# Re-pitching the state stage of a two-layer trunk: eight pairs of channel blocks, four weight tiles apart

## What is computed

```python
u = (h @ w_in)
bu = complex(einsum('blgc,gpc->blgp', ug, real(b_bar)), einsum('blgc,gpc->blgp', ug, imag(b_bar)))
_, s = associative_scan(_lin_combine, (a, bu), axis=1)
y = einsum('blgp,gcp->blgc', real(s), c_re) - einsum('blgp,gcp->blgc', imag(s), c_im)
y = y.reshape(bsz, seq, S5_WIDTH) + d * u
val, gate = split(gelu(y) @ w_out, 2, axis=-1)
x = x + val * sigmoid(gate)
```

## Time and profile before

| | us |
|---|---|
| median of 3 runs | 2246.61 (2244.24 to 2249.15) |
| the profiled execution | 2250.04 |
| its span, first to last instruction | 2248.0 |
| TensorE busy in the span | 2229.2 |
| VectorE busy | 1442.2 |
| ScalarE busy | 1021.1 |
| 1200 to 1300 us: TensorE, VectorE busy | 95.55, 83.50 |

### The profile page before, as it was taken

How to read it: one execution, slowest core, us unless ns; L and a number is a source line. 1 busy time by engine, 2 the same in 40 slices (tenths; PEclk the granted TensorE clock), 3 DMA queues, 4 the chain that set the end, 5 groups by cost and what they waited for, 6 DMA issues and landing times.

```text
span 2248.0 us, 28342 instructions
## 1 busy us (share of the span) xinstructions
PE 2229.2 (99%) x11250; PEld 1834.4 (82%) x11250; DVE 1442.2 (64%) x1590; ACT 1021.1 (45%) x1233; POOL 494.0 (22%) x469
## 2 busy tenths in 40 slices
PE   9999999999999999999999999999999999999998
PEld 7888878888888888888887788888888888888886
DVE  7878776667666666666668766555555445555665
ACT  5544454444434444445444455444444344444444
POOL 1245236455665544301003100000000000000001
PEclk9999999999999999999999999999999999999999
DMA  8667799888887888887779877677766667777764
GB/s 288 188 206 232 242 274 269 245 245 254 248 247 219 259 259 245 249 256 265 236 250 338 302 220 222 198 222 217 217 213 214 191 195 221 219 215 232 227 213 143
DMA packets 348517, 527.90 MB, mean 235 GB/s; under 512 B 105968, under 2 KB 125312, under 8 KB 347744
## 3 DMA queue, kind: packets, MB, share of 16 engines
q1 hardware_dynamic: 337296, 488.50, 71.4%
q0 software_dynamic: 8320, 30.75, 3.8%
q10 hardware_dynamic: 2768, 6.83, 0.9%
HBM read 474.10 MB, written 51.90 MB: 234 GB/s over the span
## 4 chain that ended last, share of the span: by engine, by line
PE 90%; DVE 4%; DMA 3%; issue 1%; ACT 1%; SPq 1%; DVEq 0%; ACTq 0%
PE PS L1566 58%; PE PS L1572 29%; DVE WLO L1057 1%; DMA HT<-zd 1%; DMA RAW<-in_s_w_out 1%; DMA RAW<-in_ffn_w 1%; ACT WHI L779 0%; PE PS L1597 0%; DMA RAW<-in_s_w_in 0%; PE PS L1669 0%; PE PS L1837 0%; PE PS L1838 0%; PE PS L1836 0%; DVE CB L1469 0%; PE PS L1660 0%
## 5 line engine op out<-in xcount | busy, mean ns | idle before, releaser
L1566 PE MATMUL PS<-WHI,OP 128*128 128x512 f32 x6208 | 1541.3, 390 | 1.4 <-ACT WHI L779 1.1
L1057 DVE TENSOR_TENSOR WLO<-RAW,WHI 128x1024 fp32r<-128x1024 f32 x783 | 1022.2, 1317 | 660.8 <-ACT WHI L779 657.9
L1566 PEld LDWEIGHTS PS<-WHI,OP 128*128 128x128 f32 x6208 | 1161.7, 188 | 248.1 <-issue 6.6
L779 ACT ACTIVATE WHI<-RAW 128x1024 fp32r<-128x1024 f32 x783 | 825.4, 1061 | 936.0 <-PE PS L1572 759.6
L1572 PE MATMUL PS<-WLO,OP 128*128 128x512 f32 x3104 | 830.7, 389 | 3.8 <-DVE WLO L1057 3.6
L1572 PEld LDWEIGHTS PS<-WLO,OP 128*128 128x128 f32 x3104 | 582.2, 188 | 127.1 <-DVE WLO L1057 6.1
L763 POOL TENSOR_TENSOR ON<-X,GF 128x1024 f32<-128x1024 f32 x3 | 9.9, 3291 | 947.8 <-DVE X L1406 947.8
L666 POOL TENSOR_TENSOR TA<-BRAW,FAC 128x64 f32<-128x64 f32 x16 | 8.2, 512 | 259.8 <-DMA BRAW<-in_s_b_im 259.8
L1069 DVE TENSOR_TENSOR OP<-HT,OP 128x512 fp32r<-128x512 f32 x50 | 34.9, 739 | 46.7 <-ACT OP L794 46.7
L794 ACT ACTIVATE OP<-HT 128x512 fp32r<-128x512 f32 x50 | 28.8, 624 | 65.3 <-DMA HT<-zd 65.3
L827 ACT ACTIVATE S<-PS,RC 128x512 f32<-128x512 f32 x66 | 41.8, 685 | 36.5 <-PE PS L1572 36.5
(11 more groups left out here) (213 smaller groups left out, 961.6 us busy)
## 6 DMA issues: line engine op xcount, KB each, us to landing
RAW<-in_ffn_w SPq DMA_DIRECT2D x528, 512.0 KB, 4.7
RAW<-in_gm_w_in SPq DMA_DIRECT2D x64, 512.0 KB, 4.7
RAW<-in_ple_w_gate SPq DMA_DIRECT2D x64, 512.0 KB, 4.8
RAW<-in_s_w_out SPq DMA_DIRECT2D x64, 512.0 KB, 5.2
zd<-ZT SPq DMA_DIRECT2D x37, 512.0 KB, 4.1
HT<-zd SPq DMA_DIRECT2D x148, 128.0 KB, 5.5
RAW<-in_gm_w_out SPq DMA_DIRECT2D x32, 512.0 KB, 5.3
RAW<-in_s_w_in SPq DMA_DIRECT2D x32, 512.0 KB, 6.1
```

What stands on the lines that cost most here:

```text
L779: A_.activation(hi_of(t), RAW[:, t % RING, :], ACT.Copy).then_inc(hi_ready, 1)
L1057: V_.tensor_tensor(lo_of(t), RAW[:, t % RING, :], hi_of(t).bitcast(F32), ALU.subtract).then_inc(lo_ready, 1)
L1566: T_.matmul(dst[:, th, :], x_part, WHI[:, slot, f], start=first and kk == 0 and part == 0, stop=False)
```

## The change

The eight duos had their increments 3, 5, 3, 5, 2, 6 and 2 tiles apart, and their outputs likewise. Now they stand four apart: increments at tiles 16, 20, 24, 28, 32, 36, 40, 43 and outputs at 20, 24, 28, 32, 36, 40, 44, 47. So for d = 1 to 6 the increments of duo d come right behind the outputs of duo d-1, behind the same tile. The outputs still come four tiles behind the increments of the same duo. The loads of the tables move with them, those of the last three duos' `TD` and `TK` by one to four tiles later. In `EARLY` step 4 of columns 0 and 1 goes to tiles 40 and 41 (it was at 44 and 45), and column 2 begins at tile 42 instead of 40. No instruction is added or taken away.

```diff
-EARLY = [(n, j) for j in range(4) for n in (0, 1)] + [(2, j) for j in range(4)]
-EARLY += [(n, j) for j in range(4, 8) for n in (0, 1, 2)]
+EARLY = [(n, j) for j in range(5) for n in (0, 1)] + [(2, j) for j in range(5)]
+EARLY += [(n, j) for j in range(5, 8) for n in (0, 1, 2)]
...
-INTO_AT = [W0 + g for g in (16, 19, 24, 27, 32, 34, 40, 42)]
-OUT_AT = [W0 + g for g in (20, 23, 28, 31, 36, 38, 44, 46)]
+INTO_AT = [W0 + g for g in (16, 20, 24, 28, 32, 36, 40, 43)]
+OUT_AT = [W0 + g for g in (20, 24, 28, 32, 36, 40, 44, 47)]
...
-TD_AT += [(W0 + g, W0 + g + 1) for g in (22, 26, 30, 37, 39)]
-TK_AT += [(W0 + g, W0 + g + 1) for g in (24, 30, 32, 39, 41)]
+TD_AT += [(W0 + g, W0 + g + 1) for g in (22, 26, 34, 38, 41)]
+TK_AT += [(W0 + g, W0 + g + 1) for g in (24, 30, 36, 40, 43)]
```

More of the change, by code:

```diff
@@ L183 @@
 TE_AT = [G0 + 12, G0 + 26]
-TQ_AT += [(W0 + g, W0 + g + 1) for g in (17, 20, 25, 28, 33, 35)]
-TD_AT += [(W0 + g, W0 + g + 1) for g in (22, 26, 30, 37, 39)]
-TK_AT += [(W0 + g, W0 + g + 1) for g in (24, 30, 32, 39, 41)]
-TE_AT += [W0 + g for g in (20, 23, 28, 31, 36, 38)]
+TQ_AT += [(W0 + g, W0 + g + 1) for g in (17, 21, 25, 29, 33, 37)]
+TD_AT += [(W0 + g, W0 + g + 1) for g in (22, 26, 34, 38, 41)]
+TK_AT += [(W0 + g, W0 + g + 1) for g in (24, 30, 36, 40, 43)]
+TE_AT += [W0 + g for g in (20, 24, 28, 32, 36, 40)]
 def set_before(d):
```

## The result

| | before | after |
|---|---|---|
| median, us | 2246.45 (2244.24 to 2251.0, 10 runs) | 2256.51 (2253.41 to 2258.61, 10 runs) |
| ratio | | 1.0039, 95% interval 1.003 to 1.0047 |
| the profiled execution | 2250.04 | 2257.53 |
| its span | 2248.0 | 2255.8 |

The change costs time, and +5.6 us was forecast. The medians differ by 10.1 us; the ratio, which is not that of the two medians, says 8.8, its interval 6.7 to 10.6. The busy times of the page hardly differ from the earlier trace rows (TensorE 2227.6 us, VectorE 1443.5); it counts 28344 instructions in all, two more than before, though none was added by hand.

The account below looks back on a forecast made before the run. TensorE, busy 2229.2 of 2248.0 us, was taken as the bound. New losses of 13.7 us, less 7.2 lost before, less 0.9 from joining, gave +5.6 us: 2252.2 on the median 2246.61, range 2243.5 to 2258.

Parts of the forecast that it names:

- the rival of the late loads: Table and weight loads share queue bandwidth; at 12 us a load each loop lengthens, giving 2256 to 2258 us; chance 0.13.
- The loop of VectorE: VectorE's work per duo takes 14.85 us, 16.05 with a column's transpose, against TensorE's 14.3, so VectorE falls back.
- Joining: Six pairs of outputs and increments become one group each on TensorE, saving 0.15 us a pair, 0.9 us gained.
- The walk: State stage followed in time: TensorE waits 0.8 us at tile 32, 1.1 at tile 36 and 8.0 at tile 40.
- 7 was named as a sign: On ScalarE, the spread of columns 2 and 3 comes 7 us after its store, two high parts between.
- The clock: TensorE's clock drops after the wait at tile 40; 3.4 us at half rate lose 1.7 us, ends 0 and 3.4.
- The outputs of duo 6: TensorE waits there for the transpose of the last scan: 2.1 us, between 0 and 3.
- New losses together: TensorE's new waits and low clock in the state stage: 0.8 + 1.1 + 8.0 + 1.7 + 2.1 = 13.7 us.
- 7.2 us "lost before": TensorE's loss between tile 16 and the last outputs in the old pitch: 117.3 us for 110.1 of work, taken back.
- VectorE keeps pace: Rival: the loop is nearer 14.3 us, the wait at tile 40 is 4.3; 2244.1 to 2246.2 us; chance 0.22.
- the even pitch pays: Rival: duo 4's output is ready within 9.4 us, all 7.2 and 0.9 go, 2238.5 us; chance 0.07.

Follow-up runs that it names:

- e11: The changed kernel with long-met waits added on TensorE ahead of the 100 tiles before W0; 2253.16 against 2246.76 us, ratio 1.0034.
- e3: The changed kernel with VectorE's transpose of each output ahead of the next scan, low and high passes also earlier; 2244.13 against 2245.47 us, ratio 0.9998.
- e10: e3 with two long-met waits added on TensorE ahead of each of 100 earlier tiles; 2243.66 against 2244.94 us, ratio 0.9996.
- e1: The changed kernel with step 4 of out1's columns 0 and 1 taking duo 3's output instead of duo 4's; 2252.12 against 2245.47 us, ratio 1.003.
- e7: The changed kernel with no group joined, output chain ahead of the scan, outputs taken ahead of spreads; 2244.32 against 2245.11 us, ratio 0.9993.
- e8: e3 with the outputs of duo 3 one tile earlier, so one joined group less; 2248.16 against 2245.11 us, ratio 1.0011.
- e4: The changed kernel with increments of duos 1, 3 and 5 one tile earlier, so half the groups are joined; 2252.31 against 2245.47 us, ratio 1.0032.
- e2: The kernel before with only the new order of the first columns, its old pitch kept; 2246.32 against 2245.47 us, ratio 1.0002.

## Why the prediction came out as it did

The sign, the mechanism and the place were right; the size was +10.1 us by the medians, +8.8 by the ratio, for +5.6. The median, 2256.51, lies inside the range, but 1.5 us above what the forecast gave by itself (2249.5 to 2255) and where the rival of the late loads was put (2256 to 2258). That rival is not what happened, so the number alone would point to the wrong case.

- **The loop of VectorE** (Part 2): 16 and 15, 16.5 and 15 us apart were forecast, 15.85, 14.69, 15.91 and 14.71 measured. A chain across two engines that work in order was priced from rows of before to within 0.6 us.
- **Joining**: the clean group takes 4.12 from 1198.11 to 1202.23, less 0.91 is 3.21, and 0.17 for the longer high part behind it (1.98 from 1202.23 to 1204.21, where 1.81 is usual) 3.38, against 3.56 apart: 0.18 saved, not 0.15. By the rule of the Trainium skill, "TensorEngine Tiling (Array Packing)", section "Key Properties", a drain at each change of mode, the prediction's estimate was 0.12. The trace agrees rather with a group paying once on entry and once on leaving: 1.01 us from L1775 to L1783 and 1.09 on to L1758, as in a group apart.
- **The walk** (Part 3): tiles 32 and 36 were not waited for (0.8 and 1.1 forecast), and tile 40 for 6.0 rather than 8.0. Here a step was missing: TensorE's pauses, 2.4 us from start to start of what lies around them from duo 2 on, made it come later to a chain that didn't wait for it. Wait and pauses are 8.4, for 9.9 forecast. The store on ScalarE also held less than thought: it landed in 5.9 us at the median and not 7.6, and the spreads came 6.3 us behind it for column 2 and 5.6 for column 3, where 7 was named as a sign.
- **The clock**: 2.0 for 1.7, though the second trace of after lost 2.9 by it. **The outputs of duo 6**: 2.2 for 2.1.
- **New losses together**: 6.0 + 2.4 + 0.7 (the pause in duo 1's increments) + 2.0 + 2.2 = 13.3, for 13.7 forecast; joining gave 1.1, for 0.9.
- **The term that failed is the 7.2 us "lost before".** The walk was made against the one trace, and against that trace it holds: 13.3 less 7.2 less 1.1 is +5.0, and the length went from 258.8 to 263.7, +4.9. But that trace is the longest of three. On their mean the stage lost 5.7 and not 7.2, and at the shortest 3.7; so the change takes back less: +6.5, between 4.9 and 8.6. The prediction took the trace's 3.4 us above the median as a constant to be taken off, when part of it was just the loss that the change removes.
- **What stays open**: from 6.5 in the stage to 8.8 by the ratio and 10.1 by the medians. The ratio of e11, whose stage is after's, says 7.6 (5.6 to 9.9); the two intervals share 6.7 to 9.9, and the traces' 4.9 to 8.6 overlap with that. Part of the gap may be no more than scatter. That the stage of before is nearer to 255.4 in the executions not profiled would explain the rest, and isn't shown.

Of the rivals, "VectorE keeps pace" fell with the spacing of the scans, "the even pitch pays" with the transpose behind the scan; e3 shows its condition was named rightly, that an output taken early saves the loss, but not its price: e3 is level with before and not 8.1 us below. "Loads come late" fell: loads of `w_out` tiles landed in 6.3 us at the median in the stage, 8.8 before.

## What to carry to other kernels

Before evening out the pitch of a pipeline, walk the order of each in-order engine once around the loop: a small operation that lands behind a long one (a transpose of 0.7 us behind a scan of 6.3) sets when all behind it is ready. In the old pitch the scan of duo 5 stood ahead of the outputs of duo 4; evening the pitch put it between these outputs and their transpose. Take the loss that a change should remove from several traces, since waits of this kind vary by microseconds from one execution to another, and the first trace may be at an end. Experiments that take one idle time away say little unless the late engine is helped: in e10 shorter pauses came back as a longer wait, in e1 most of the wait came back as a pause and a low clock. And before an idle time is put down to "issue", see what ended just ahead of its end: in e7 and e8 it was a scan.

## What the hardware showed that was not expected

- A dense run of small matmuls outran its instructions. Packets of 16 KB on the instruction queue, 89 in the whole program, each taking 0.9 to 1.2 us where it was looked at, stand for 127 matmuls with their weight loads. Where 160 small matmuls ran in 3.3 us, TensorE paused in some places, not in all, for 0.5 to 3.7 us until 2.2 to 2.7 us behind such a packet's start; in the three traces of before, with groups of 64 and 96 matmuls and whole tiles between them, none was seen. The Trainium skill, "Runtime: NRT & Kernel Launch", section "Instruction fetch mechanics", has the blocks of 16 KiB or 256 instructions, and the trace agrees with 127 to 128 pairs; that the refill is hidden by the rate of issue didn't hold here.
- The wait at tile 40, some 6 us, brought the granted clock to 0.50 for 7 to 10 us in the two traces of after, of which 2.7 and 4.1 passed within the wait itself, and cost 2.0 and 2.9 us more; in e11 it cost 1.6. After 3.49 in e4 the same tile's high part took 3.44, but after 1.49 in e2 and 1.04 in e1 only 2.11 and 2.06, nearly the usual 1.98. The length of the idle time alone doesn't tell: behind 1.81 us in e1 and 2.28 in e8 the granted clock fell to 0.50, behind 2.58 in e10 it stayed at 1.00.
